# One hybrid decoder step on one core: the first product of the merge as a phase of its own, in pairs of weight tiles by one Strassen level

## The reference

```
h = rmsnorm(x, g_pre)
z = h @ w_in                       # (tokens, 1024) @ (1024, 4544)
q_lat, kv_lat, k_r, z_att, u_pool, z_pool, g_att, g_pool = jnp.split(z, SPLIT_POINTS, axis=-1)
...                                # latent attention of q over ckv_new / cache -> o_lat (8 heads of 128)
o = jnp.einsum('bshr,rhv->bshv', o_lat, w_uv).reshape(b, L, ATT_WIDTH)
y_att = (o * jax.nn.silu(z_att)) @ w_o_att
p, pool_state = pool_mixer(u_pool, pool_hist, pos, w_pool, pool_scale)   # windows 2, 4, 8, 16
y_pool = (p * jax.nn.silu(z_pool)) @ w_o_pool
merged = jax.nn.sigmoid(g_att) * y_att + jax.nn.sigmoid(g_pool) * y_pool
x = x + merged @ w_out             # then the final rmsnorm
```

## Time and profile before

| | us |
|---|---|
| median of 3 runs | 2118.76 |
| lowest, highest | 2118.68, 2119.72 |
| span of the profiled execution, first to last instruction | 2117.8 |
| `project` and start of `attend` | 0 to about 195 |
| `attend` | to about 820 |
| `decode` | to about 880 |
| `merge` | to the end |

### The profile page before, as it was taken

How to read it: one execution, slowest core, us unless ns; L and a number is a source line. 1 busy time by engine, 2 the same in 40 slices (tenths; PEclk the granted TensorE clock), 3 DMA queues, 4 the chain that set the end, 5 groups by cost and what they waited for, 6 DMA issues and landing times.

```text
span 2117.8 us, 31439 instructions
## 1 busy us (share of the span) xinstructions
PE 2080.6 (98%) x11893; PEld 1949.3 (92%) x11893; DVE 1279.8 (60%) x2689; ACT 971.8 (46%) x1729; POOL 354.0 (17%) x499
## 2 busy tenths in 40 slices
PE   6999999999999999999999999999999999999997
PEld 5999888888888887799999999999999999999997
DVE  6786878778878775465444643455444644446434
ACT  4446666566555555543334423343334433344333
POOL 3444211011101101240004100050002300041000
PEclk9999999999999999999999999999999999999999
DMA  8876321111110305445343453444534453334532
GB/s 299 262 230 181 99 61 46 31 31 31 30 31 17 118 11 191 131 132 183 120 141 115 137 176 118 142 127 146 162 108 144 137 178 120 126 118 126 175 119 73
DMA packets 159844, 260.44 MB, mean 123 GB/s; under 512 B 21354, under 2 KB 109810, under 8 KB 158662
## 3 DMA queue, kind: packets, MB, share of 16 engines
q1 hardware_dynamic: 153758, 237.59, 36.0%
q0 software_dynamic: 2304, 12.58, 1.6%
q10 hardware_dynamic: 3632, 8.28, 1.2%
HBM read 216.97 MB, written 41.66 MB: 122 GB/s over the span
## 4 chain that ended last, share of the span: by engine, by line
PE 56%; DVE 1%; DMA 0%; ACT 0%; issue 0%; ACTq 0%; POOLq 0%; POOL 0%; DVEq 0%
PE b_ps L122 56%; PE b_ps L2104 1%; DMA d_ws<-in_w 0%; DVE d_y L1992 0%; ACT d_wr L1245 0%; DVE d_y L2012 0%; DVE d_wr L84 0%; DVE d_y L1994 0%; ACT d_y L1893 0%; POOLq L1623 0%; ACTq L1623 0%; ACT d_zs L1886 0%; ACT d_zs L1869 0%; DVE d_gate_p L2020 0%; DVE d_pool L84 0%
## 5 line engine op out<-in xcount | busy, mean ns | idle before, releaser
L122 PE MATMUL b_ps<-d_ht,d_wr 128*128 128x412 f32 x3840 | 734.8, 350 | 2.0 <-DVE d_wr L84 1.7
L122 PEld LDWEIGHTS b_ps<-d_ht,d_wr 128*128 128x128 f32 x3840 | 715.8, 188 | 6.1 <-issue 2.8
L84 DVE TENSOR_TENSOR d_wr<-d_ws,d_wr 128x1024 fp32r<-128x1024 f32 x260 | 322.0, 1238 | 550.6 <-ACT d_wr L1245 550.4
L1245 ACT ACTIVATE d_wr<-d_ws 128x1024 fp32r<-128x1024 f32 x260 | 275.0, 1058 | 601.9 <-PE b_ps L122 591.9
L750 PE MATMUL b_ps<-kt,k_qs 128*128 128x512 f32 (+2 forms) x1520 | 337.3, 370 | 0.0
L750 PEld LDWEIGHTS b_ps<-kt,k_qs 128*128 128x128 f32 x1520 | 265.7, 188 | 45.6 <-DVE b_p L1094 0.7
L84 DVE TENSOR_TENSOR b_pt<-b_ps,b_pt 128x512 fp32r<-128x512 f32 x272 | 183.4, 689 | 91.8 <-ACT b_pt L1048 90.5
L1048 ACT ACTIVATE b_pt<-b_ps 128x512 fp32r<-128x512 f32 x272 | 158.4, 597 | 166.7 <-PE b_ps L1154 116.7
L1154 PE MATMUL b_ps<-b_pt,kv 128*128 128x512 f32 x816 | 227.8, 408 | 0.0
L1041 ACT ACTIVATE b_p<-b_p,b_bias 128x1024 f32<-128x1024 f32 (+7 forms) x192 | 171.6, 897 | 54.4 <-DVE b_low L1101 53.5
L122 PE MATMUL b_ps<-d_mrg,d_wr 128*128 128x412 f32 x960 | 189.8, 353 | 0.0
(11 more groups left out here) (212 smaller groups left out, 2059.5 us busy)
## 6 DMA issues: line engine op xcount, KB each, us to landing
d_ws<-in_w SPq DMA_DIRECT2D x260, 512.0 KB, 3.6
out_q<-a_qout SPq DMA_DIRECT2D x32, 384.0 KB, 3.9
d_hf<-out_ht SPq DMA_DIRECT2D x20, 412.0 KB, 3.6
d_olf<-out_olat SPq DMA_DIRECT2D x40, 206.0 KB, 2.9
a_xt<-in_x_t SPq DMA_DIRECT2D x16, 512.0 KB, 5.2
out_ht<-a_hf SPq DMA_DIRECT2D x16, 512.0 KB, 3.8
out_olat<-b_ol SPq DMA_DIRECT2D x32, 256.0 KB, 4.2
out_y<-d_y SPq DMA_DIRECT2D x5, 1536.0 KB
```

The source lines that it names most:

```text
L84: return e.tensor_tensor(low, source, high.bitcast(f32), ALU.subtract)
L122: mm = pe.matmul(out, stationary(a, k), moving(b, k), start=first and k == 0 and a + b == 0, stop=last and k == depth - 1 and a == 1)
L1245: act.activation(ahead["wr"][k % 2][:, 0, :, :], ahead["ws"][k % 4][:, :, :], ACT.Copy).then_inc(ahead["w_hi"], 1)
```

## The change

The merge becomes two phases. The first makes only the first product, in NAP = 4 passes of TA = 516 tokens (two halves of HA = 258), over 16 pairs of weight tiles: (U, ZP), (ZA, ZA), (GA, GP). A pair, the two halves of its depth and the two halves of the tokens are a 2 x 2 by 2 x 2 product; one level of Strassen's scheme in Winograd's form makes it of 7 products instead of 8, each 4 depth blocks x 3 matmuls of 258 columns.

- Seven operands of a product are sums. Those of h (`h_sums`, 4 GpSimd operations per depth block) are made anew for each pass, and all seven forms of h are split (`h_high`, `h_low`: 258, 516 and 1032 columns per depth block). Those of the weights are made once: GpSimd adds quarters of tiles during `attend` (16 x 4 operations of 128x512), SP loads the quarters and stores the sums to scratch.
- The products are accumulated partly in PSUM, partly by evictions (ACT: p1, u2, u3) and additions (DVE: three of 258 columns per pair).
- The unit of weights is half a tile (128 x 512): loads run 6 ahead, splits 3 ahead.
- The gates and silu(z_att) are stored to scratch (`zs`, `sa`, `sp`, `gp`) and loaded again in the second phase, which has 5 chunks of 412 tokens as before with only OA, OP and WO.
- In `decode`, h of the first pass is prepared in steps 4 to 7, the weights only after the last transposes, and only one product of 12 matmuls is issued there.

The core of the diff (memory layout and unchanged bodies left out):

```
+HD = KD // 2
+NAP, HA = 4, 258
+TA = 2 * HA
+PAIRS = 2 * NG + KD
+UNIT = HD * P
...
             for u in range(SMALL + 2, units):
                 load(u)
                 store(u - 6)
+                if FIRST_SUMS <= u < FIRST_SUMS + PAIRS:
+                    load_quarters(u - FIRST_SUMS)
+                if FIRST_SUMS < u <= FIRST_SUMS + PAIRS:
+                    store_sums(u - FIRST_SUMS - 1)
...
+            def add_quarters(n):
+                pool.wait_ge(q_ok, n + FIRST_SUMS + 2)
+                pool.wait_ge(pair_io[n % 2], 32 * (n // 2) + 16)
+                of, to = quarters[n % 2], sums[n % 2]
+                pool.tensor_tensor(to[:, 0, :], of[:, 2, :], of[:, 3, :], ALU.add).then_inc(added, 1)
+                pool.tensor_tensor(to[:, 2, :], of[:, 0, :], of[:, 2, :], ALU.subtract).then_inc(added, 1)
+                pool.wait_ge(added, 4 * n + 1)
+                pool.tensor_tensor(to[:, 1, :], to[:, 0, :], of[:, 0, :], ALU.subtract).then_inc(added, 1)
+                pool.wait_ge(added, 4 * n + 3)
+                pool.tensor_tensor(to[:, 3, :], of[:, 1, :], to[:, 1, :], ALU.subtract).then_inc(added, 1)
...
+def slot_order():
+    slots = []
+    for g in range(NAP * PAIRS):
+        slots += [(g, 1), (g, 2)]
+        if g:
+            slots.append((g - 1, 4))
+        slots += [(g, 6), (g, 5)]
+        if g:
+            slots.append((g - 1, 3))
+        slots.append((g, 7))
...
+WS, WR, LEAD = 6, 4, 3
...
+def unit_high(act, ahead, s):
+    act.wait_ge(ahead["w_in"][s % WS], (QUERY if s % WS < 4 else 0) + 16 * (s // WS + 1))
+    act.activation(ahead["wr"][s % WR][:, 0, :, :], ahead["ws"][s % WS][:, :, :], ACT.Copy).then_inc(ahead["w_hi"], 1)
+
+def unit_low(dve, ahead, s):
+    dve.wait_ge(ahead["w_hi"], s + 1)
+    split(dve, ahead["wr"][s % WR][:, 1, :, :], ahead["ws"][s % WS][:, :, :],
+          ahead["wr"][s % WR][:, 0, :, :]).then_inc(ahead["w_ok"], 1)
...
+            for s, (g, p) in enumerate(SLOTS):
+                act.wait_ge(unit_ok, s + 1)
+                if p == 1:
+                    wait(act, added, add_count[g - 1, 7] if g else 0)
+                    act.activation(p1[:, :], bank[A_BANK[g % 2]][:, 0:HA], ACT.Copy).then_inc(evicted, 1)
...
+                if p == 7:
+                    act.wait_ge(added, add_count[g, 2])
+                    act.activation(u3[:, :], bank[A_BANK[g % 2]][:, 0:HA], ACT.Copy).then_inc(evicted, 1)
+                unit_high(act, ahead, s + LEAD)
+                if s == 1:
+                    act.wait_ge(const_in, 64)
...
+                if p == 4:
+                    second_result(g)
+                if p == 7 and g and kind_of(g - 1) != "U":
+                    first_result(g - 1)
+                if p == 2 and g in H_STEP:
+                    h_high(act, ahead, H_STEP[g])
...
+            for s, (g, p) in enumerate(SLOTS):
+                dve.wait_ge(unit_ok, s + 1)
+                if p == 2:
...
+                    dve.tensor_tensor(first_sum(g)[:, 0:HA], bank[C_BANK][:, 0:HA], p1[:, :], ALU.add).then_inc(added, 1)
+                if p == 3:
+                    dve.tensor_tensor(first_sum(g)[:, HA:TA], bank[B_BANK[g % 2]][:, 0:HA], u2[g % 2][:, :],
+                                      ALU.add).then_inc(added, 1)
+                unit_low(dve, ahead, s + LEAD)
+                if p == 7:
+                    dve.wait_ge(evicted, evict_count[g, 7])
+                    dve.tensor_tensor(c22[g % 2][:, :], bank[B_BANK[g % 2]][:, 0:HA], u3[:, :], ALU.add).then_inc(added, 1)
...
+                if p == 6 and g and kind_of(g - 1) != "GA":
+                    second_product(g - 1)
+                if p == 1 and g >= 2 and kind_of(g - 2) == "ZA":
+                    first_product(g - 2)
+                if p == 5 and g in H_STEP:
+                    h_low(dve, ahead, H_STEP[g])
```

## The result

The changed kernel takes 2224.11 us (median of 4 runs, 2223.61 to 2228.26) against 2118.93 before: ratio 1.050, 95% interval 1.0487 to 1.0517. It is 105 us slower; I had forecast 2082, 37 us faster. The profiled execution has a span of 2222.1 us against 2117.8, so 104.3 us are to be found.

A forecast was written before the change was run, and what follows sets the result against it. TensorE, busy 98% of 2117.8 us, was taken as the bound. Terms -68.8 + 6 + 19 + 0 + 0 + 1 + 3 + 3 = -37 us took 2118.8 to 2082 us; own range 2070 to 2100, with rivals 2055 to 2120.

The forecast's parts named there:

- Price of a matmul: New first product: a 258-column matmul costs 121 ns from start to start, against 187.4 ns for 412 columns.
- rival 4: New phase: weight load not hidden behind a short matmul sets the spacing, 188 ns; about 2417 us; chance 0.01.
- Starts of products: First product: more, shorter products each start with a wait of 16 ns; +6 us, bounds 0 and 12.
- First product, saving: Merge: 3900 matmuls (730.9 us) replaced by 5472 shorter ones (662.1 us); -68.8 us.
- Feeding TensorE: New phase: stalls on ACT and DVE preparing splits, including 6 us for GpSimd's windows; +19 us, bounds 0 and 60.
- h in the wrong groups: New phase: DVE's h_low delays the low part in twelve groups that prepare h; 10 us of the stalls.
- DMA: New phase: 230 GB/s needed, 296 reached earlier, loads issued early enough; nothing charged.
- rival 3: New phase: DMA supplies less than 230 GB/s; 2161 us at 200 GB/s; chance 0.08.
- Second phase: Merge's later chunks: 99.4 us each remain, ACT and DVE fit within a half tile; nothing charged.
- Attention: Attention: 64 added GpSimd operations fit, slowing some DVE work, and SP waits for sums; +1 us, bounds 0 and 10.
- Decode: Decode: preparing h takes more ACT and DVE time in steps 4 to 7; +3 us.
- Rival 2: New phase: serial c22, eviction, high and low part exceed the margin in every group; 2100 to 2120 us; chance 0.13.

The follow-up runs named there:

- experiment 4: Changed kernel with TensorE's pool product issued two products later, its gating and store later by as much; 2187.28 us.
- experiment 7: Changed kernel, seven moves: sums' transfers, pool product and constants' wait later, h groups, y/x queue order, additions later in the unit, weight loads 6 to 8 earlier; 2080.44 us.
- experiment 1: Changed kernel with SP's loads of weight quarters and stores of their sums in attention two units later; 2152.65 us.
- experiment 2: Changed kernel with GpSimd's 64 additions in attention on one column only, sums left out of the computation; 2181.22 us.
- experiment 3: Changed kernel with the sums' transfers two units later and the additions in attention on one column; 2135.18 us.

## Why the prediction was wrong

- **Price of a matmul** (121 ns, bounds 120.3 and 123.2): right. 744 in 89.82 us are 120.7. The rule of the Trainium skill on which rival 4 drew (page "TensorE: Matmul & The Clock Gate": section "LDWEIGHTS (loading the stationary operand)", a load of 128 columns takes 107 ns; section "The mechanism", it overlaps a matmul in flight only when the row group differs) would give 214; the trace disagrees again.
- **Starts of products** (+6 us): nothing. The 120.7 ns contain 62 starts. The 16 ns that I took from before were no constant of a start.
- **First product, saving** (-68.8): there, in the gate pairs; eaten by what follows.
- **Feeding TensorE** (+19, bounds 0 and 60): mis-sized. 743.6 - 662.1 - 4.5 = 77.0 us lie over the matmuls, where starts, stalls and the merge's start were to be 28. The step that failed is that I worked out the hand-off of weights alone. The split of pooled is a second one, on the same engine, with one product of time for about 1.9 us of DVE's work; I counted the pool product as 96 matmuls and nothing else. Its place cost 41.6 us (experiment 4), 29.2 in idle time and 12.4 in clock. The terms that I did work out were fair: h in the wrong groups 10 us forecast, 9.8 measured together with the constants' wait; windows 6 forecast, 14 in the changed kernel and 6.4 in the kernel of experiment 7; the merge's start 3 forecast, 4.1 for the loads 6 to 8 alone. The last lies within the stage's spread of 5 us, the others not far above it.
- **The clock** (no term). I took 1.00 for the stretches before the change and let it stand for after: every stall was priced at its idle time alone. It fell to 0.95 in attention and 0.98 in the new phase, and the same matmuls were busy 21.8 and 12.4 us longer than without the stalls.
- **DMA** (0, rival 3): right. ACT's high parts waited 356.5 of their 358.7 us for TensorE, none to speak of for d_ws, with 233 GB/s in the fed stretch 1090 to 1180.
- **Second phase** (0): +8.5. A wait of SP for y held up the next load; that half tiles left it less cover than whole ones had is my reading, not tested. I had charged nothing without reading SP's list there.
- **Attention** (+1, bounds 0 and 10): here the prediction failed, by 83 us. I had seen the wait: "SP now waits for these sums ahead of its next query load; that load still has most of a unit". The query had its unit, mostly; but I asked only for the next entry in the queue. The entry behind it, the store of the output, had less cover: two buffers, and ACT in order behind them. And I measured the wait from the 5 us of the additions, not from the moment at which GpSimd could begin them, which hangs on a query two units on. Of the 84.2 us the new place in the queue gives back 70 (experiment 1), of which some 31 needed the additions' length too (experiment 2); 14 are contention (experiment 3). All of it is gone in experiment 7.
- **Decode** (+3): +3.4, right in size. TensorE's waits for DVE's copies of keys there went from 2.3 to 4.2 us, as I had it; what makes up the rest I did not look for.
- **Rivals.** The slower rival that I priced was DMA supply; what came was a queue. Rival 2, "the handoff becomes the bound", came closest: true of half of each pass, and for another hand-off.

That the seventh kernel takes 2080 us, near the forecast, confirms the matmul term and the absence of a DMA limit in the new phase. That it is so near is partly luck: its first product gains 47.3 us where 40.8 were forecast, and its second phase loses 3.7 where none were. And it is a kernel with seven waits and steps in other places.

## What to carry to other kernels

When a change puts a wait into an in-order queue, go through every entry behind it for one whole round, and for each ask whose buffer it frees and how many there are; and date the wait by when its producer can begin, not by how long it takes. When the steps of a pipeline get shorter, list every hand-off that is counted in steps, the small ones too: a distance of "one product" was 4.5 us before and 1.45 after. Work for an idle engine is free only in the right part of the unit: the same 64 additions cost 14 us beside DVE work that touches only SBUF and nothing where little of that was under way. And price a stall of TensorE at more than its idle time: in attention 62.4 idle us brought 21.8 more in clock, in the new phase 29.2 brought 12.4.

## What I had not expected of the hardware

- A DVE addition of one column (128x1) took 1.25 us while GpSimd was adding; the least and the median are 0.14 and 0.16. Before the change the longest, beside GpSimd's split of a query, was 1.04. A 128x1024 product with one wide operand, in SBUF, took 1.64 us instead of 0.75. The gating product that reads PSUM and SBUF kept its 0.41 us beside the windows (L2239), its neighbour with two SBUF operands went to 1.16 (L2240). The Trainium skill, page "GPSIMD Engine Reference", section "Specifications", names as contending with GpSimd the DVE instructions in a 2-port mode or with two SBUF inputs; the trace agrees, and it adds that even a single column can wait about as long as one GpSimd addition of 1.3 us lasts.
- TensorE's clock is lost along with the feeding: 1.00 before and in experiment 7, 0.95 over attention and 0.80 in the stretch with 12 idle us in 40. The longest 128x512 matmul of attention's last product took 776 ns in the changed kernel, twice the least (388), and 485 before and in experiment 7. Matmuls of over 600 ns of that product stand in four places, at 425, 461, 676 and 711 us, and each time TensorE had just stood idle, for 8.4, 9.5, 2.4 and 2.4 us: after such a wait the next matmuls ran at the lower of the two levels.
